# First expert block's rows taken from SBUF by one-hot products instead of a gather

## The reference, cut to what matters

```
h = rms_norm(x, g) * (1.0 + scale2) + shift2
top_p, top_i = lax.top_k(jax.nn.softmax(e_logits, axis=-1), 2)   # e_logits of the best group
hid = silu(h @ w_gate[e]) * (h @ w_up[e])                        # 256 wide, for each chosen e
x = x + gate2 * sum_over_chosen(gate * (hid @ w_down[e]))
```

## Time and profile before

| | us |
|---|---|
| median of 3 runs | 760.4 (759.92 to 761.41) |
| span of the profiled execution, its own time | 768.8 |
| load 5 issued by SP, in the profiled execution | 522.77 |
| first gather issued by POOL | 519.30 |
| block 0's gate/up begins | 525.83 |

### The profile page before, as it was taken

One profiled execution on the slowest core, in us unless ns is written; L12 is line 12 of the kernel. 1 busy time (PEld: TensorE's weight loads), 2 busy tenths in 40 slices (PEclk: granted clock), 3 DMA queues, 4 the chain that ended last, 5 costly groups with the idle time before them and its releaser, 6 DMA issues.

```text
span 768.8 us, 11131 instructions
## 1 busy us (share of the span) xinstructions
PE 739.2 (96%) x4235; PEld 464.7 (60%) x4235; DVE 409.4 (53%) x942; ACT 205.8 (27%) x418; POOL 171.1 (22%) x193
## 2 busy tenths in 40 slices
PE   7999999999999999998999999989999999999986
PEld 5445465688756567885888444656555555555541
DVE  4124399998999998600254235974432232222235
ACT  5012253306467675002000011222111111111112
POOL 2031021240000000073400004543333333333210
PEclk9999999999999999998999999989999999999999
DMA  8973064113255275443232842377999999999988
GB/s 339 419 254 97 0 218 159 46 78 115 109 220 220 110 256 207 143 166 138 80 116 83 344 179 92 139 260 286 423 423 425 427 424 423 426 426 422 423 332 321
DMA packets 29385, 187.72 MB, mean 244 GB/s; under 512 B 7264, under 2 KB 8352, under 8 KB 17936
## 3 DMA queue, kind: packets, MB, share of 16 engines
q1 hardware_dynamic: 18880, 164.98, 53.9%
q0 software_dynamic: 9536, 19.72, 7.8%
q10 hardware_dynamic: 912, 2.26, 0.8%
HBM read 180.89 MB, written 16.13 MB: 256 GB/s over the span
## 4 chain that ended last, share of the span: by engine, by line
PE 75%; DVE 9%; DMA 8%; issue 3%; ACT 2%; SPq 1%; POOL 1%; DVEq 0%; ACTq 0%; POOLq 0%
PE psum L810 23%; PE psum L1302 13%; PE psum L777 12%; PE psum L1316 7%; DMA ring<-in_experts 5%; PE psum L724 3%; PE psum L1295 2%; DMA ring<-in_stream 2%; PE psum L670 2%; DMA ring<-expert_rows 1%; DVE arena L2284 1%; DVE arena L2282 1%; DVE arena L2283 1%; PE psum L653 1%; PE psum L1309 1%
## 5 line engine op out<-in xcount | busy, mean ns | idle before, releaser
L810 PE MATMUL psum<-hT,ring 128*128 128x260 f32 x640 | 146.7, 389 | 5.3 <-issue 3.3
L810 PEld LDWEIGHTS psum<-hT,ring 128*128 128x128 f32 x640 | 121.9, 192 | 29.5 <-issue 8.5
L1785 ACT ACTIVATE arena<-psum 128x512 f32<-128x512 f32 (+10 forms) x127 | 68.3, 573 | 234.8 <-PE psum L653 50.9
L777 PE MATMUL psum<-ring,hT 128*128 128x512 f32 (+1 forms) x256 | 93.1, 517 | 0.0
L777 PEld LDWEIGHTS psum<-ring,hT 128*128 128x128 f32 x256 | 47.4, 190 | 41.8 <-issue 32.6
L1302 PE MATMUL psum<-ring,arena 128*64 128x256 f32 x608 | 69.0, 379 | 2.2 <-DMA ring<-in_experts 1.2
L1316 PE MATMUL psum<-arena 128*64 128x512 f32 x280 | 67.8, 605 | 1.4 <-issue 1.4
L1717 POOL DMA_INDIRECT expert_rows<-arena,router x34 | 34.5, 1014 | 140.0 <-DVE arena L2784 127.7
L1302 PEld LDWEIGHTS psum<-ring,arena 128*64 128x64 f32 x608 | 43.8, 137 | 31.3 <-issue 10.3
L2777 DVE COPY arena<-psum 128x128 f32<-128x128 f32 x35 | 10.2, 291 | 95.6 <-PE psum L1309 83.8
L810 PE MATMUL psum<-arena,ring 128*128 128x260 f32 x256 | 58.9, 386 | 0.0
(11 more groups left out here) (398 smaller groups left out, 962.5 us busy)
## 6 DMA issues: line engine op xcount, KB each, us to landing
ring<-in_stream SPq DMA_DIRECT2D x21, 2048.0 KB, 8.9
ring<-in_experts SPq DMA_DIRECT2D x16, 2048.0 KB
arena<-in_experts SPq DMA_DIRECT2D x32, 1024.0 KB
arena<-in_experts SPq DMA_DIRECT2D x11, 2048.0 KB
hT<-in_experts SPq DMA_DIRECT2D x5, 2048.0 KB
ring<-expert_rows SPq DMA_DIRECT2D x8, 512.0 KB, 7.2
ring<-in_stream SPq DMA_DIRECT2D x2, 1280.0 KB, 6.1
arena<-in_x_prompt SPq DMA_DIRECT2D x4, 512.0 KB, 5.7
```

Of the source, the lines that this page charges most:

```text
L777: mm = pe.matmul(psum[:, b, 0:width], hT[:, k, t * P:(t + 1) * P], w[:, k, :], start=(k == 0), stop=(k == KD - 1))
L810: mm = pe.matmul(psum[:, b0 + s, 0:HALF], w[:, k, f * P:(f + 1) * P], rhs[:, k, s * HALF:(s + 1) * HALF], start=(first and k == 0), stop=( ...
L1785: ins = act.activation(out, in_, func, scale=scale)
```

## The change

Block 0's rows no longer come through HBM. `to_slots` writes for each tile which of its rows sit in the first expert's slots, as a one-hot (`first_hot`) multiplied by the row's root. `first_rows` multiplies the residual rows with it, tile by tile, into one PSUM bank; ACT copies it out, PE turns it into bank 0, and DVE multiplies each of the eight pieces by `scale_T` and adds what `first_samples` gave: the samples' normed rows and the prompt's shift, by a one-hot and its complement. The samples' normed rows therefore move to partitions 64 to 71 of `x2`, and the shift is broadcast to partitions 64 to 127 by one more DMA of POOL. `gate_up` of block 0 waits for each piece. The gathers begin with block 1. The adaLN spreads, `gate_sums` 3 and 4 and several waits change their place, and the filler products `idle5` to `idle7` are gone. SP's load 5 waits for the samples' spread (`adaS` 10, now behind block 0's `gate_up` on PE) and for the gather of block 1.

```diff
 @@ PE
+            def first_samples(*ks):
+
+                if ks[0] == 0:
+                    pe.wait_ge(*first_hot_ready(1))
+                    pe.wait_ge(t2_ready, 2)
+                    banks.begin(pe, "first_s", 0)
+                for k in ks:
+                    f = 4 * (k % 2) + k // 2
+                    mm = pe.matmul(psum[:, 0, k * SB:(k + 1) * SB], x2[HD:P, NT, f * P:(f + 1) * P], first_hot_s[HD:P],
+                                   start=True, stop=True)
+                if ks[-1] == KD - 1:
+                    banks.filled(mm, "first_s")
+
+            def first_rows(t):
+
+                pe.wait_ge(*first_hot_ready(ROUTE.index((P, t))))
+                if t == 0:
+                    banks.begin(pe, "first", 1)
+                for h in range(2):
+                    mm = pe.matmul(psum[SB * h:SB * h + SB, 1, :], first_hot[:, t, :], x2[:, t, 512 * h:512 * h + 512],
+                                   start=(t == 0), stop=(t == NT - 1), tile_position=(0, SB * h))
+                if t == NT - 1:
+                    banks.filled(mm, "first")
...
             places(3)
             gate_sums(2)
+            first_samples(0, 1, 2)
             x2_transposes(4)
             pick_sums(3)
 
             router_logits(4)
-            wide_spread(10, 0)
-            samples_spread(10, 2, 1)
-            wide_spread(11, 5)
+            first_samples(3, 4, 5, 6, 7)
+            for t in range(NT - 1):
+                first_rows(t)
             places(4)
...
-            keep_busy("idle5", 4, 3)
+            gate_sums(3)
+            wide_spread(10, 0)
+            wide_spread(11, 5)
+            first_rows(NT - 1)
             pick_sums(4)
-            keep_busy("idle6", 4, 2)
+
+            banks.wait_drained(pe, "first")
+            banks.wait_drained(pe, ("adaP", 10))
+            for c in range(4):
+                mm = pe.transpose(psum[:, 0, c * P:(c + 1) * P], y_rows[:, 1, c * P:(c + 1) * P], ident)
+            mm.then_inc(xT_full, 1)
...
-            gate_sums(3)
-            gate_sums(4)
-            keep_busy("idle7", 6, 16)
-            for name in ("order", "tables", ("adaP", 10), ("adaP", 11), ("adaS", 10)):
-                banks.wait_drained(pe, name)
-            pe.wait_ge(x_got[0], 16)
-            x_transposes(0, 0, xT_full)
-
...
-                    gate_up(p, w_gu[pos % BUFFERS], gu_full)
+                    gate_up(p, w_gu[pos % BUFFERS], gu_full, first=(b == 0))
                     if b == 0:
+                        gate_sums(4)
+                        samples_spread(10, 2, 1)
+                        for name in ("order", "tables", ("adaP", 11)):
+                            banks.wait_drained(pe, name)
                         gate_items()
                         over_code()
+                        banks.wait_drained(pe, ("adaS", 10))
 @@ SP
-            banks.wait_full(sp, ("adaP", 11))
-            sp.wait_ge(x_got[0], 16)
+            banks.wait_full(sp, ("adaS", 10))
+            sp.wait_ge(*rows_got(1))
             banks.wait_drained(sp, "order")
             banks.wait_full(sp, "gate_sums")
             load_gate_up(5, 5, gu_got[5])
 @@ POOL
+            pool.wait_ge(*shift_scale_in)
+            pool.dma_start(x2[HD:P, NT, :].rearrange("p (c n) -> p c n", c=2),
+                           by_group[MODS.index("shift2"), NS].partition_broadcast(P - HD)).then_inc(late_in, 16)
...
-            for b in range(X_BUFFERS):
+            for b in range(1, X_BUFFERS + 1):
                 gather(b)
 @@ ACT
             exponents(3)
+            evac("first_s", [(x_T[:, 0], psum[:, 0, :].rearrange("p (k n) -> p k n", k=KD))])
             t2_store(4)
...
+            exponents(4)
             gate2_out(10, 0)
-            evac(("adaS", 10), [(gate2_s[0:NS, 512 * g:512 * g + 512], psum[32 * g:32 * g + NS, 1, :]) for g in range(2)])
-            exponents(4)
             gate2_out(11, 5)
+            evac("first", [(y_rows[:, 1, :], psum[:, 1, :])])
 @@ DVE
+                lane.mark(dve.tensor_scalar(of_first[0:n, t], expert_f[0:n, t], 0.0, None, ALU.is_equal))
...
+                lane.then(dve.scalar_tensor_tensor(junk32[0:n, 0:2], place[0:n, t], 1.0, of_first[0:n, t], ALU.add, ALU.mult,
+                                                   accum_out=first_slot[0:n, t:t + 1]))
+                by_order = lambda a: a.rearrange("p (a m j) -> p a m j", a=2, m=8)
+                if t < NT:
+                    dve.tensor_scalar(by_order(first_hot[:, t, :]), slot_order, first_slot[:, t:t + 1], rstd[:, t:t + 1],
+                                      ALU.is_equal, ALU.mult).then_inc(c_silu, 1)
+                else:
+                    lane.then(dve.tensor_scalar(by_order(first_hot_s[s_rows]), slot_order[0:n], first_slot[0:n, t:t + 1],
+                                                None, ALU.is_equal))
+                    dve.tensor_scalar(first_hot_s[s_shift], first_hot_s[s_rows], -1.0, 1.0 / NS, ALU.mult, ALU.add)\
+                       .then_inc(c_silu, 1)
...
+            dve.wait_ge(xT_full, 1)
+            banks.wait_drained(dve, "first_s")
+            for k in range(KD):
+                f = 4 * (k % 2) + k // 2
+                dve.scalar_tensor_tensor(x_T[:, 0, k, :], psum[:, 0, k * SB:(k + 1) * SB], scale_T[:, f:f + 1],
+                                         x_T[:, 0, k, :], ALU.mult, ALU.add).then_inc(x_scaled, 1)
```

More of the change, by code:

```diff
@@ L1296, in x_transposes, with gate_up @@
                 mm.then_inc(full, 1)
-            def gate_up(p, w, full):
+            def gate_up(p, w, full, first=False):
                 for k in range(KD):
+                    if first:
+                        pe.wait_ge(*first_xT(k))
                     for half in range(2):
@@ L1667, in shifted @@
                 n, t = ROUTE[i]
-                out = t2[i % 2][0:n]
+                out = t2[i % 2] if t < NT else normed_s
+                shift = mod2["shift2"][0] if t < NT else mod2["shift2"][1][s_rows]
                 pool.wait_ge(scaled2, i + 1)
-                pool.tensor_tensor(out, out, mod2["shift2"][t == NT][0:n], ALU.add).then_inc(t2_ready, 1)
+                if t == NT:
+                    pool.wait_ge(t2_ready, i)
+                pool.tensor_tensor(out, out, shift, ALU.add).then_inc(t2_ready, 1)
+                if t == NT:
+                    pool.wait_ge(t2_ready, i + 1)
             def to_gates(i):
@@ L2080, in _ @@
                 silu(p, silu_done)
+                if b == 0:
+                    evac("gate_sums", [(gate_table[0:NE],
+                                        spread_dim(psum[0:NE, 7, 0:P].rearrange("p (h n) -> p h n", h=2), 2, 2))])
+                    evac(("adaS", 10), [(gate2_s[0:NS, 512 * g:512 * g + 512], psum[32 * g:32 * g + NS, 1, :])
+                                        for g in range(2)])
+                    banks.wait_drained(act, ("adaS", 10))
+                    act.dma_start(kept_rows[0], gate2_s[0:NS, :]).then_inc(s_kept[0], 16)
                 if b + 1 < N_MAIN:
@@ L2467, in _ @@
             lane.mark(dve.memset(gate_of, 0.0))
+            lane.mark(dve.memset(first_hot_s[HD:P], 0.0))
             def modulated2(n, rows):
@@ L2541, in second_norm @@
                 n, t = ROUTE[i]
-                out = t2[i % 2][0:n]
+                out = t2[i % 2] if t < NT else normed_s
                 dve.wait_ge(rstd2_ready, i + 1)
+                if t == NT:
+                    dve.wait_ge(late_in, 32)
                 if i >= 2:
@@ L2784, in y_scaled @@
                 dve.tensor_tensor(y_rows[:, p, :], psum[:, 6 + p, :], y_rows[:, p, :], ALU.mult).then_inc(done, 1)
-            for name in (("adaP", 10), ("adaP", 11), ("adaS", 10)):
-                banks.wait_drained(dve, name)
             over_blocks()
@@ L2810, in _ @@
                         dve.wait_ge(*zeros_stored)
+                        for name in (("adaP", 10), ("adaP", 11)):
+                            banks.wait_drained(dve, name)
                     elif b >= 3:
```

48 lines of the change are left out of this document (28 added, 20 removed).

## The result

The changed kernel takes 768.5 us (20 runs) beside 763.2 us for the kernel before (20 runs): ratio 1.0061, 95% interval 1.0044 to 1.0078, so 3.4 to 6.0 us slower, 4.7 in the middle. The forecast stood on a median of three runs, 760.4; over 20 runs the kernel before has 763.2, so the measured 768.5 lies 3.5 us above the range's end of 765.0. Even on the old base, 760.4 x 1.0061 = 765.04 is just past that end. The forecast shift of +1.6 was 3 us short.

A forecast was written before the change was run, and what follows sets the result against it. The prediction took the stream of expert weights to bound the kernel: load 5's delay 4.3, less 2.4 for closed holes and 0.25 for the dropped gather, gives +1.65 us on 760.4, so 762.0 us; range 758.5 to 765.0.

The forecast's parts named there:

- X: How much later than 522.77 us SP issues load 5; forecast 4.3 us, break-even 2.65.
- the holes: Two gaps in the weight stream between loads 5, 6 and 7; closing them was to gain 2.4 us.
- gather 0's traffic: Block 0's gather no longer made, some 0.1 MB less in the DMA queue; was to gain 0.25 us.
- PE up to the fifth tile's places: Second part of load 5's delay: new products behind the last logits make the places +2.3 us late, bounds 1.5 to 3.
- third rival: PE at the 1.2 GHz level during block 0's gate/up, load 5 about 5 us later than forecast: 767 us; chance 0.10.
- DVE to the choice: First part of load 5's delay: added VectorE work until the last tile is routed, 1.6 us, bounds 0.8 to 2.4.
- From places to gather 1: Third part of load 5's delay: from the places at 514.6 through products, turning, scaling and token table to 523.6 us.
- from gather 1 to load 5: From gather 1's issue to SP's load 5, taken as 3.47 us like gather 0 before: load 5 at 527.1.
- The removed fillers: Filler products idle5 to idle7 on PE; claimed to have held nobody but PE, so removing them costs nothing.
- Additions mostly hidden: Rival: added DVE and PE work falls into existing waits, load 5 only 2.6 to 3.3 late: 760.7 us; chance 0.19.
- PE sets the end: Rival: the end follows PE's blocks, starting 3.0 us earlier, not the weight stream: 757.4 to 760.4 us; chance 0.18.
- Slow clock: Rival: half clock on block 0's gate/up, 7.3 instead of 3.67 us there: 767 us or less; chance 0.10.

The follow-up runs named there:

- e11: The changed kernel profiled again without an edit; load 5 at 70.0 and last gate/up at 289.6 us after load 2; the changed kernel's ratio is 1.0061.
- e12: The changed kernel profiled a third time without an edit; load 5 at 70.1 and last gate/up at 289.3 us after load 2; the changed kernel's ratio is 1.0061.
- e3: The changed kernel with one wide spread moved back directly behind the last logits; ratio to the kernel before 1.0019.
- e8: The changed kernel with three filler products in front of the last tile's transposes; ratio to the kernel before 1.0030.
- e16: Third profile of the changed kernel with three filler products before the last tile's transposes; last gate/up 288.2 us after load 2; that kernel's ratio is 1.0030.
- e14: The kernel before profiled a third time without an edit, no half clock around the change; load 5 at 64.7 and last gate/up at 284.1 us after load 2.
- e7: The kernel before with ten instead of sixteen filler products in idle7; ratio to the kernel before 0.9971.
- e10: The kernel before with six instead of sixteen filler products in idle7; ratio to the kernel before 0.9999.
- e1: The kernel before with SP made to wait for block 0's gate/up ahead of load 5; ratio to the kernel before 1.0052.
- e6: The changed kernel with gate_sums 4 and sample spread before gate/up 0, token table before scaled pieces, one wide spread behind the last logits; ratio to the kernel before 1.0004.
- e13: The kernel before profiled again without an edit; load 5 at 63.8 and last gate/up at 284.8 us after load 2.
- e9: The changed kernel with most first_rows, all first_samples, turning and scaling moved behind the tables, off the way to gather 1; ratio to the kernel before 1.0026.
- e15: Second profile of the changed kernel with three filler products before the last tile's transposes; last gate/up 289.6 us after load 2; that kernel's ratio is 1.0030.

## Why the prediction was wrong

**The mechanism held.** The end follows the weight stream; loads 5 and 6 leave together; no hole is left; the last blocks wait for weights more often and longer; the shift is X minus what the holes cost. With the profiles' own numbers X = 71.86 - 65.08 = 6.78 and the holes with gather 0's traffic 221.29 - 219.20 = 2.09, which makes +4.69. That this is the shift of the last gate/up is so by construction; that the timed runs, +4.7, agree so closely with one pair of profiles is luck, since three profiles of each kernel spread by 2.3 and 1.8 us. Both terms were mis-sized.

**X: the step that failed is "PE up to the fifth tile's places".** Forecast +2.3 with bounds 1.5 to 3; measured 60.30 - 54.59 = +5.7 in this profile and +4.0 in e11 and e12. In it the twelve `first_rows` were priced at 2.8 and took 5.39 (4.49, 4.49), the ten `first_samples` at 1.25 and took 1.96 (1.33, 1.33). The durations at full clock were right (2.79 in e3, e8 and e16; in e8 and e16 the places come at 57.5, +2.9). The third rival had the mechanism, half clock over new work on the path, and put it at gate/up 0 with a chance of 0.10; it reasoned that PE is busy before the products. The rows show it there all the same.

**The rest of X was right.** DVE to the choice +2.1 (+1.9 in e11 and e12) for 1.6. The Trainium skill's page "SBUF — State Buffer" (section "Who interferes with whom") would add the accumulate of two SBUF operands beside POOL's addition: it took 1.96 beside POOL's 2.35 and 0.16 where POOL was idle, so the rule held on this row; its 0.3 would have put the choice at 1.9. From places to gather 1 8.7 for 9.0; from gather 1 to load 5 2.9 for 3.5. At full clock, with the three fillers, load 5 leaves at 69.0 (e8, e16); the forecast, 65.08 + 4.3, was 69.4.

**The holes: -2.4 was read from an execution with half clock in it.** Means of three executions: load 5 64.52 before and 70.67 after, X = 6.15; last gate/up 285.1 and 290.0, +4.9. Behind load 5 stood 220.6 us before and 219.3 after, so closing the holes gave 1.2, not 2.4 + 0.25. The forecast's error of 3.3 us on this basis is 1.4 of the holes, 1.7 of half clock, and 0.2 of all other steps. This split is an estimate: 1.7 is 70.67 against 69.01 in e8 and e16, which have the three fillers; the changed kernel itself was never seen without half clock. Wholly at full clock (e16 against e14) the change costs 4.1 us, X 4.3 less 0.2: there X is what was forecast, and the whole error is the credit for the holes.

Two sentences of the forecast fall with it. The removed fillers did hold more than PE: load 6 stood behind them (e7, e10). And block 1's gate/up was to end 3 us earlier; it ends at 78.03 after load 2, before at 78.05.

**The rivals.** "Additions mostly hidden": no, the choice was 2.1 late and the places later still. "PE sets the end": no, PE's blocks were not earlier at all, and e1 gave PE its old start and lost 0.5%. "Slow clock": right mechanism, wrong place; and the stretch in the kernel before was taken for a fixed part of it. Half clock varies between executions, and only six of before and changed were profiled: where it strikes in the timed runs is not known, only its sum, and the agreement of +4.9 with the measured +4.7 is of means over three.

**A better version.** e6 comes nearest to before (1.0004, interval to 1.0024); no changed order was shown to beat it.

## What to carry to other kernels

Before adding up a shift, look for a stretch at half clock in the profile of before, and ask which of the waits and holes that the change is to remove exist only because of it; several profiled executions of the unchanged kernel answer this, three of which halve the credit here (1.2 for 2.65); a second one alone could have been e13, with a hole as large from another place. Where a queue of loads sets the end, new work is paid as far as it moves the load from which the queue runs without a hole, however idle the engines are later. That load can change: in e9 load 5 went out early and load 7 became the late one. New products on that way are priced at either clock, since PE's half clock may fall on any of them.

## What the runs showed of the hardware

- The place of the half clock is not a property of the instruction order: around the change three executions of the kernel before had 7 us of it over small products, 3.5 us over a gate/up (5.36 us instead of 3.67), and none; three of the kernel with fillers (e8, e15, e16) had none, 7 us in two pieces, and none. The waits of PE in the 10 us ahead of such a stretch were short, 0.84 and 0.35 us in the first profile of the changed kernel.
- One instruction of 512 columns with 128 x 64 weights, half of a product of the program, took 0.23 us at full clock (2.79 for twelve) and 0.45 at half clock (5.39 for twelve). The twelve that had one 3.5 us stretch over part of them took 4.49.
- A DVE accumulate over 128x2 took 1.96 us beside POOL's 2.35 us addition and 0.16 alone: the size of the instruction doesn't protect it.
- The way from gather 0's issue to load 5's was 3.47, 3.43 and 4.37 us in three executions of one kernel (before, e13, e14), at full clock in the last two: a landing of a small gather varies by about a microsecond.
